# First normalisation of a two-layer hybrid trunk step, transposed before it is modulated

## The chip, the cores and the metric

One core of a Trainium2 chip runs the whole program. The metric is device time in microseconds. Engines are called PE (TensorE; PEld is its weight load), DVE (VectorE), ACT (ScalarE), POOL (GpSimd) and SP (SyncE); a name with a q behind it (SPq, ACTq) is that engine's sequencer, which issues DMAs.

## What is computed

Two trunk layers over 640 tokens (128 context tokens, 512 latent tokens) of width 1024. Each sub-layer begins with a normalisation and a modulation by learned columns, and its result goes through a projection. Only the first one matters here:

```python
def ada_params(cvec, w_mod, b_mod):
    m = jax.nn.silu(cvec) @ w_mod + b_mod
    return jnp.split(m[:, None, :], N_MOD, axis=-1)
...
hp = modulate(rmsnorm(xp, norm_mix_pre[layer]), mod_p[0], mod_p[1])   # x * (1 + scale) + shift
hs = modulate(rmsnorm(xs, norm_mix_pre[layer]), mod_s[0], mod_s[1])
u, v, gate, xr = jnp.split(h @ w_in, [D_A, 2 * D_A, 2 * D_A + D_RG], axis=-1)
```

The modulation vectors are `silu(c) @ w_mod`: a 1024 x 6144 weight per layer, of which shift and scale of the first sub-layer are 2 x 1024 columns, 8 MB. Context tokens and latent tokens have vectors of their own.

## The kernel before

`schedule()` writes out by hand one list of steps (`STEPS`) and one list of weight loads of 1 MB (`LOADS`). Each engine's block walks the whole list of steps in order and does its own part of each; semaphores join them. So the order of the list is the order of work on PE, DVE, ACT and POOL alike. SP walks the list of loads in order: a load that waits for its buffer holds all behind it.

**Products.** Large products are made in three passes (`split3`, L1146): an f32 operand is cut into a high part (fp32r) and a remainder, and high x high, high x remainder and remainder x high are accumulated. Weights are cut by `split`: ACT copies a block of 128 x 1024 to `WH` (L630), POOL subtracts it and writes `WL` (L854). `RING` holds 6 such blocks. A step's `split` list names the blocks cut behind it. Activations are cut alike into `HH` and `HL`, features on the partitions, 8 feature tiles by 640 tokens.

**Loads.** `RAW` has two buffers (`RAWN`). A load into a used one waits on SP until its old content is read: for a first half of modulation weights until PE has multiplied it (`mod_read`, L582), for a weight pair until POOL has cut it (`w_lo`, L586). Six loads behind the first two (`EARLY`, L397) go to memory that is free at the start and wait for nothing. The input tokens `X` are loaded from ACT's queue (L614, L615).

**Modulation.** A step `mod` (L1177) multiplies two loads (16 matmuls of 128 x 512 with 32 columns of weights), DVE copies the bank to `PART` (L932), and the step `modfin` transposes it on PE (L1210) and lets DVE sum it into `MODC` and add bias and gain (L948 to L957). Four such pairs, `mod(0, 0, 0)`, `mod(0, 0, 1)`, `mod(0, 1, 0)` and `mod(0, 1, 1)`, give shift (c = 0) and scale (c = 1) of the first sub-layer, in halves of 512 features.

**Normalisation.** `pre` (L674, L969) squares and sums a tile of 128 tokens on ACT (L681), takes the root (L682), and DVE scales the tile into `ACC` (L973). `T` (L974, L1212) transposes its 8 feature tiles on PE in two banks; DVE modulates the lower four out of PSUM into `HF` (L982), ACT the upper four (L695). `cut` (L684) casts them into `HH` on ACT (L700, L702); DVE and POOL write the remainders to `HL` (L988, L849). `HF` is one buffer, so tile t + 1 is modulated only when tile t is cut.

**The first pair.** `apair("xr", 0, ...)` multiplies two blocks of 128 columns of `w_in` with all tokens, in two ranges, 0:256 and 256:640, each over the whole K of 8 feature tiles: the first range when two token tiles are cut, placed between tiles 3 and 4; the second when all are. `apair("xr", 2, ...)` and `apair("gate", 0, ...)` follow.

In order, the list before begins:

```python
mod(0, 0, 0)
step("sheet", uses_m=1)
mod(0, 0, 1)
P_(0, 0)
mod(0, 1, 0)
P_(0, 1)
...
```

The steps that the prediction speaks of by line: L681, L682, L972, L973 (`pre`), L1221 (transposes of `T`), L1189 (`mod`), L1210 and L948 to L957 (`modfin`), L630 and L854 (weights cut), L988 and L849 (remainders), L1149 to L1151 (`split3`), L576 and L589 (SP's loads).

Of the kernel before, what the change touches and what calls it, by code (L numbers as in the profile page):

```python
# [28 lines left out]
RAWN = 2  # L29
RING = 6  # L30
# [6 lines left out]
def schedule():  # L37
# [32 lines left out]
    def mod(layer, c, half):  # L70
        flush()
        ld = load("mod", layer=layer, c=c, half=half, kh=0, n=cb[0])
        load("mod", layer=layer, c=c, half=half, kh=1, n=cb[0])
        step("mod", uses_m=1, layer=layer, c=c, half=half, ld=ld, n=cb[0])
        pend.append((layer, c, half, cb[0]))
        cb[0] += 1

    def apair(what, tile, src, col, part=None, ld=None, norm=0):

        if ld is None:  # L80
            ld = load("acols", src=src, col=col)
        j = loads[ld]["first"]
        if part == 0:
            return step("A", uses_a=0, what=what, tile=tile, j=j, parts=(0,), fin=False, norm=norm), ld
        return step("A", uses_a=2, frees=2, what=what, tile=tile, j=j, parts=(1,) if part == 1 else (0, 1), fin=True, norm=norm), ld

# [72 lines left out]


    mod(0, 0, 0)
    step("sheet", uses_m=1)
    mod(0, 0, 1)
    P_(0, 0)
    mod(0, 1, 0)
    P_(0, 1)
    P_(0, 2)
    mod(0, 1, 1)
    P_(0, 3)
    P_(0, 4)  # L170
    flush()
    steps[-1]["split"] = [0, 1]
    for t in range(TT):
        T_(0, t)
        if t == 4:
            steps[-1]["split"] = [2, 3, 4, 5]
        if t == 3:
            ld = apair("xr", 0, ("w_in",), 1536, 0)[1]
    step("lambda")
    apair("xr", 0, ("w_in",), 1536, 1, ld)  # L180
    apair("xr", 2, ("w_in",), 1536 + 256)
# [123 lines left out]
def hybrid_step(nc, A):  # L305
# [5 lines left out]
    with ctx:  # L311
# [11 lines left out]
        X = sb("X", [P, TT, D])  # L323
        EARLY_H = alias("EARLY_H", [P, 4, 2048])
        HH = sb("HH", [P, KD, TOK], f32r)
# [60 lines left out]
        PT_LOAD = next(i for i, ld in enumerate(LOADS) if ld.get("src") == ("w_out_odd",)) + 1  # L386
        PT = [RAW[:, PT_LOAD % RAWN, 512 * i:512 * i + 512] for i in range(4)]

# [5 lines left out]
        def k_tok(t):  # L394
            return KTOK[:, {0: 0, TT: 1}.get(t, 2 + t % 2), :]

        EARLY = {i: EARLY_H[:, i - RAWN, :] if i < RAWN + 4 else MX[:, 2048 * (i % 2):2048 * (i % 2) + 2048]  # L397
                 for i in range(RAWN, RAWN + 6)}


        early_in = [sem(f"early_in{i}") for i in range(6)]
        raw_in = [sem(f"raw_in{i}") for i in range(RAWN)]
        const_in = [sem(f"const_in{i}") for i in range(14)]
        w_hi, w_lo, mod_read = sem("w_hi"), sem("w_lo"), sem("mod_read")
# [120 lines left out]
        def raw_arrived(eng, ld):  # L525
            if ld in EARLY:
                eng.wait_ge(early_in[ld - RAWN], 16)
            else:
                eng.wait_ge(raw_in[ld % RAWN], 16 * ((ld - (len(EARLY) if ld >= RAWN else 0)) // RAWN + 1))

# [19 lines left out]
        def raw(i):  # L550

            return EARLY[i] if i in EARLY else RAW[:, i % RAWN, :]

# [18 lines left out]
        @block.sync  # L572
        def _(sp):
            for i, ld in enumerate(LOADS):
                if i in EARLY:
                    sp.dma_start(raw_dst(i, ld), dram_view(ld)).then_inc(early_in[i - RAWN], 16)  # L576
                    continue
                if i >= RAWN:

                    old = LOADS[i - RAWN - (len(EARLY) if i < 2 * RAWN + len(EARLY) else 0)]  # L580
                    if old["kind"] == "mod" and old["kh"] == 0:
                        sp.wait_ge(mod_read, old["n"] + 1)  # L582
                    elif old["kind"] == "mod":
                        upto(sp, m_ready, old["m"])
                    else:
                        sp.wait_ge(w_lo, old["first"] + 2)  # L586
                    if i == PT_LOAD + RAWN:
                        upto(sp, m_ready, PV_M[-1])
                sp.dma_start(raw_dst(i, ld), dram_view(ld)).then_inc(raw_in[i % RAWN], 16)  # L589

            for t in range(TT):
                sp.wait_ge(x_new, 3 * TT + t + 1)
                dst = A["y_prompt"][0] if t == 0 else A["y_sample"][0, (t - 1) * P:t * P, :]
                sp.dma_start(dst, X[:, t, :]).then_inc(stored, 16)
            sp.wait_ge(stored, 16 * (2 + TT))
            sp.wait_ge(k_out, 16)
# [3 lines left out]
        def _(act):  # L600
# [6 lines left out]

            xs = A["x_sample"][0].rearrange("(t p) n -> p t n", p=P)
            act.dma_start(CC[:, 0, :], A["c_ctx"].rearrange("(p k) -> p k", k=KD)).then_inc(const_in[3], 16)
# [3 lines left out]
            act.dma_start(IDN[:, :], A["ident"]).then_inc(const_in[5], 16)  # L613
            act.dma_start(X[:, 0, :], A["x_prompt"][0]).then_inc(const_in[0], 16)  # L614
            act.dma_start(X[:, 1:TT, :], xs).then_inc(const_in[1], 16)  # L615

# [16 lines left out]
            for s in STEPS:  # L633
# [40 lines left out]
                elif k == "pre":  # L674
                    ph, t = s["ph"], s["t"]
                    if ph:
                        act.wait_ge(x_new, (ph - 1) * TT + t + 1)
                    else:
                        act.wait_ge(const_in[0] if t == 0 else const_in[1], 16)
                        act.wait_ge(consts_made, 3)  # L680
                    link(nc.scalar.activation(JUNK, X[:, t, :], ACT.Square, accum_out=STAT[:, t, 3:4]))  # L681
                    nc.scalar.activation(STAT[:, t, 4:5], STAT[:, t, 3:4], ACT.Sqrt, scale=1.0 / D, bias=EPSC[:, :])\  # L682
                        .then_inc(xsum, 1)
                elif k == "cut":  # L684

# [17 lines left out]
                elif k == "A" and s["fin"]:  # L703
                    if s["what"] == "xr" and s["tile"] == 2:

                        input_ready(act, TT)
                        act.dma_start(WSR, A["gmlp_ws"][0].rearrange("h p q -> p h q")).then_inc(wst_in, 16)
# [84 lines left out]
                elif k == "Q":  # L792
                    u, i = s["m"], s["n"]
                    act.wait_ge(m_ready[u % 2], u // 2 + 1)
                    if i == 0:
                        input_ready(act, 3 * TT)
                    if i > 1:
# [61 lines left out]
        def _(dve):  # L859
# [40 lines left out]
            for s in STEPS:  # L900
# [241 lines left out]
        def _(pe):  # L1142
# [21 lines left out]

            RANGE = ((0, 256), (256, TOK))
            ntiles = ngate = 0
            for s in STEPS:
# [31 lines left out]
                elif k == "modfin":  # L1199
                    upto(pe, m_free, MOD_M[s["n"]])  # L1200
                    if s["c"] in (2, 5):
                        for v in (0, 1):
                            u = s["m"] + v
                            m_acquire(u)
                            MM(m_bank(u), SEL[:, v, :], PART[:, :], start=True, stop=True).then_inc(m_ready[u % 2], 1)
                    else:
                        u = s["m"]
                        m_acquire(u)
                        for i in range(4):
                            ins = TR(m_bank(u)[:, P * i:P * i + P], PART[:, P * i:P * i + P], IDN[:, :])  # L1210
                        ins.then_inc(m_ready[u % 2], 1)
                elif k == "T":  # L1212
                    ntiles += 1
                    t = s["t"]
                    pe.wait_ge(xn_ready, s["n"] + 1)
                    for q in (0, 1):
# [6 lines left out]
                elif k == "A":  # L1223

                    for part in s["parts"]:
                        if len(s["parts"]) == 1:
                            input_ready(pe, ntiles if part else TT * s["norm"] + 2)
                    if len(s["parts"]) == 2:
                        input_ready(pe, ntiles)
# [25 lines left out]
                elif k == "B":  # L1255
                    b, t, nb, what = s["b"], s["t"], s["nb"], s["what"]
                    b_acquire(b)
                    if what == "wout":
                        if s["ph"] == 1 and nb == 0:
                            pe.wait_ge(mix_lo, 4)  # L1260
                            upto(pe, m_free, YA_M[t])
                        if s["ph"] == 3:
                            upto(pe, m_free, PV_M[-2])
                            upto(pe, m_free, PV_M[-1])
                    elif what == "qkv":
                        input_ready(pe, 2 * TT + (t + 1 if nb == 2 else TT))
                    for kt in range(KD):
# [177 lines left out]
```

## Time and profile before

| | us |
|---|---|
| median of 3 runs (1629.41 to 1630.31) | 1629.56 |
| the profiled execution, its own time | 1628.96 |
| its span | 1627.2 |
| PE busy | 1506.1 (93%) |
| DVE / ACT / POOL busy | 656.2 / 554.5 / 518.1 |
| DMA moved | 153.87 MB, mean 95 GB/s |
| mean granted clock of PE | 0.968 |

The span runs from the first to the last instruction; the profiled execution's own time is 1.76 us more. In rows of the trace each line has its start and its busy time in us, the engine, the line of the kernel, the operation, the tiles it writes and reads (`out<-in`), how many instructions are merged in it (x4), and in brackets how long the engine was idle before it and what ended that. Granted clock 1.00 is 2.4 GHz, 0.50 is 1.2 GHz.

### The profile page before, as it was taken

What the parts mean: (1) busy time and instruction counts of PE and PEld (TensorE: products, weight loads), DVE (VectorE), ACT (ScalarE), POOL (GpSimd) and SP (SyncE); (2) the same over time, 40 slices, a digit from 0 to 9 for tenths busy, and PEclk for the clock granted to TensorE, in tenths of its full rate; (3) what the DMA queues carried; (4) which work ended last, traced back from release to release, by engine and by line L of the source; (5) the groups of instructions that cost most, each with busy time, mean ns of one, the idle gap of its engine ahead of it and who ended that gap; (6) DMA issues with size and microseconds to landing.
All of it is one profiled execution on the core that took longest, in us unless ns stands there. A gap on an engine that the chain in (4) does not pass through costs nothing.

```text
span 1627.2 us, 20069 instructions
## 1 busy us (share of the span) xinstructions
PE 1506.1 (93%) x8338; PEld 1242.4 (76%) x8338; DVE 656.2 (40%) x1124; ACT 554.5 (34%) x927; POOL 518.1 (32%) x224
## 2 busy tenths in 40 slices
PE   4799869899999999999889789989899999999997
PEld 1786646697898898998677656657689899989985
DVE  3665662733322322222644466623542232223225
ACT  3456732631221221232531266614532223222211
POOL 0521233141242243243234134413324234323330
PEclk9899979999999999999999899999899999999999
DMA  9322425144344342222022000033242122213201
GB/s 336 98 78 104 145 70 174 37 158 143 130 141 144 130 152 93 92 78 78 27 83 78 27 1 2 1 104 130 82 145 84 59 97 79 78 52 104 78 26 65
DMA packets 90498, 153.87 MB, mean 95 GB/s; under 512 B 6356, under 2 KB 44704, under 8 KB 90408
## 3 DMA queue, kind: packets, MB, share of 16 engines
q1 hardware_dynamic: 81712, 143.14, 26.7%
q10 hardware_dynamic: 8696, 9.45, 2.1%
q8 instruction: 66, 1.08, 0.3%
q14 instruction: 24, 0.20, 0.0%
HBM read 149.69 MB, written 2.89 MB: 94 GB/s over the span
## 4 chain that ended last, share of the span: by engine, by line
PE 71%; DVE 8%; ACT 5%; issue 2%; DMA 1%; POOL 1%; ACTq 0%; DVEq 0%; SPq 0%
PE PS L1149 20%; PE PS L1150 20%; PE PS L1151 20%; PE PS L1189 3%; PE PS L1387 2%; PE PS L1379 1%; DVE X L968 1%; DVE ACC L967 1%; PE PS L1357 1%; PE PS L1340 1%; PE PS L1358 1%; POOL WL L854 1%; ACT XCB L671 1%; DVE HL L988 1%; DVE HF L982 1%
## 5 line engine op out<-in xcount | busy, mean ns | idle before, releaser
L854 POOL TENSOR_TENSOR WL<-RAW,WH 128x1024 fp32r<-128x1024 f32 x172 | 422.0, 2484 | 769.2 <-ACT WH L630 769.2
L1149 PE MATMUL PS<-HH,WH 128*128 128x384 f32 (+1 forms) x1152 | 359.6, 312 | 10.4 <-DVE HL L988 5.3
L1151 PE MATMUL PS<-HH,WL 128*128 128x384 f32 (+1 forms) x1152 | 358.2, 311 | 0.0
L1150 PE MATMUL PS<-HL,WH 128*128 128x384 f32 (+1 forms) x1152 | 358.2, 311 | 0.0
L630 ACT CAST WH<-RAW 128x1024 fp32r<-128x1024 f32 x172 | 170.3, 1047 | 500.5 <-PE PS L1151 294.4
L1149 PE MATMUL PS<-WH,AH 128*128 128x512 f32 x640 | 253.3, 396 | 11.8 <-DVE AL L1003 6.5
L1150 PE MATMUL PS<-WL,AH 128*128 128x512 f32 x640 | 251.3, 393 | 0.0
L1151 PE MATMUL PS<-WH,AL 128*128 128x512 f32 x640 | 251.1, 392 | 0.0
L1149 PEld LDWEIGHTS PS<-HH,WH 128*128 128x128 f32 x1152 | 221.3, 192 | 16.1 <-issue 9.8
L1150 PEld LDWEIGHTS PS<-HL,WH 128*128 128x128 f32 x1152 | 221.5, 192 | 0.5
L1151 PEld LDWEIGHTS PS<-HH,WL 128*128 128x128 f32 x1152 | 220.9, 192 | 0.0
L1070 DVE TENSOR_TENSOR ACC<-ACC,PS 128x512 f32<-128x512 f32 x140 | 95.6, 687 | 233.3 <-PE PS L1151 233.3
L1001 DVE TENSOR_TENSOR XCB<-XCB 128x640 f32<-128x640 f32 x64 | 65.7, 1027 | 288.7 <-ACT XCB L718 288.5
L1149 PEld LDWEIGHTS PS<-WH,AH 128*128 128x128 f32 x640 | 121.1, 189 | 47.2 <-issue 8.6
L1149 PE MATMUL PS<-WH,HH 128*128 128x512 f32 x360 | 147.7, 410 | 8.7 <-POOL WL L854 5.4
L1150 PE MATMUL PS<-WL,HH 128*128 128x512 f32 x360 | 142.7, 396 | 0.0
L1151 PE MATMUL PS<-WH,HL 128*128 128x512 f32 x360 | 142.6, 396 | 0.0
L1151 PEld LDWEIGHTS PS<-WH,AL 128*128 128x128 f32 x640 | 121.3, 189 | 25.8
L1150 PEld LDWEIGHTS PS<-WL,AH 128*128 128x128 f32 x640 | 121.2, 189 | 24.7 <-issue 0.2
L718 ACT ACTIVATE XCB<-PS 128x640 f32<-128x640 f32 x64 | 45.1, 705 | 199.7 <-PE PS L1151 199.7
L1003 DVE TENSOR_TENSOR AL<-XCB,AH 128x640 fp32r<-128x640 f32 x64 | 76.7, 1198 | 50.7 <-ACT AH L724 50.7
L1149 PEld LDWEIGHTS PS<-WH,HH 128*128 128x128 f32 x360 | 69.1, 192 | 35.4 <-issue 10.9
(160 smaller groups left out, 1552.3 us busy)
## 6 DMA issues: line engine op xcount, KB each, us to landing
RAW<-in_w_mod SPq DMA_DIRECT2D x42, 1024.0 KB, 5.1
RAW<-in_w_ffn_in SPq DMA_DIRECT2D x32, 1024.0 KB, 5.7
RAW<-in_w_ffn_out SPq DMA_DIRECT2D x32, 1024.0 KB, 4.9
RAW<-in_w_in_even SPq DMA_DIRECT2D x8, 1024.0 KB, 6.8
RAW<-in_w_qkv SPq DMA_DIRECT2D x6, 1024.0 KB, 5.4
EARLY_H<-in_w_mod SPq DMA_DIRECT2D x4, 1024.0 KB, 21.2
RAW<-in_w_out_even SPq DMA_DIRECT2D x4, 1024.0 KB, 5.5
RAW<-in_w_out_odd SPq DMA_DIRECT2D x4, 1024.0 KB, 5.2
```

Of the source, the lines that this page charges most:

```text
L630: nc.scalar.copy(ring_view(WH, ld, j), w_view(ld, b)).then_inc(w_hi, 1)
L671: link(nc.scalar.activation(JUNK, ACC[:, t, :], ACT.Square, accum_out=STAT[:, t, 0:1]))
L718: nc.scalar.activation(XC[0], a_bank(a), ACT.Relu).then_inc(a_free[a % 2], 1)
L854: nc.gpsimd.tensor_tensor(ring_view(WL, ld, j), w_view(ld, b), ring_view(WH, ld, j).bitcast(f32), ALU.subtract).then_inc(w_lo, 1)
L1001: V_.tensor_tensor(XC[1], XC[0], XC[0], ALU.mult).then_inc(sq_ready, 1)
L1003: V_.tensor_tensor(AL[:, slot, :], XC[1], AH[:, slot, :].bitcast(f32), ALU.subtract).then_inc(a_lo, 1)
L1070: V_.tensor_tensor(acc, acc, bank, ALU.add).then_inc(b_free[b % 2], 1)
L1149: MM(out, wh, xh, start=first, stop=False)
L1150: MM(out, wh, xl, start=False, stop=False)
L1151: return MM(out, wl, xh, start=False, stop=last)
L1189: ins = MM(PS[32 * kt:32 * kt + 32, 6 + u % 2, :], CL[:, 4 * kh + kt, :], rv[:, kt, :], start=(kh == 0), stop=(kh == 1 and not gate))
L1387: ins = MM(PS[64 * par:64 * par + 64, 6 + u % 2, 0:256], vv(keys[kt])[:, HD * g:HD * g + HD], pt[:, par, :, :], start=(kt == 0), stop=(kt ...
```

## The change

The input tokens are loaded first, from SP's queue, tile by tile. Each tile is normalised as before and then transposed unmodulated: `xt` transposes its 8 feature tiles into two banks, DVE copies the lower four and ACT the upper four back to `ACC`. All five tiles come ahead of the modulation. Then the modulation pairs run in another order: first the lower half of the features (shift, scale), then the upper half. A new step `h0` per feature tile modulates all 640 tokens on DVE (two instructions, context and latent), casts on ACT and writes the remainder on DVE, in place of POOL and DVE by token tile. The first pair of products is made in two halves of K: `A0` over feature tiles 0 to 3 of block 0 ahead of the upper modulation pairs and of block 1 behind them, then tiles 4 to 7 of both (`kh=1`).

The list of loads becomes: 0, 1 (shift, lower), 2, 3 (scale, lower), 4 (the first `w_in` pair), 5, 6 (shift, upper), 7, 8 (scale, upper), 9 (next `w_in` pair), and so on. 2, 3, 5, 6, 7 and 8 are the ones with memory of their own; 0 and 1 take the two RAW buffers, 4 takes the buffer of 0, 9 that of 1.

```diff
+    for t in range(TT):
+        P_(0, t)
+        step("xt", t=t)
+    step("sheet", uses_m=1)
     mod(0, 0, 0)
-    step("sheet", uses_m=1)
+    mod(0, 1, 0)
+    flush()
+    ld = load("acols", src=("w_in",), col=1536)
+    steps[-1]["split"] = [0]
+    for f in range(4):
+        step("h0", f=f)
+    steps[-1]["split"] = [1]
+    step("A0", i=0, j=0)
     mod(0, 0, 1)
-    P_(0, 0)
-    mod(0, 1, 0)
-    P_(0, 1)
-    P_(0, 2)
     mod(0, 1, 1)
-    P_(0, 3)
-    P_(0, 4)
     flush()
-    steps[-1]["split"] = [0, 1]
-    for t in range(TT):
-        T_(0, t)
-        if t == 4:
-            steps[-1]["split"] = [2, 3, 4, 5]
-        if t == 3:
-            ld = apair("xr", 0, ("w_in",), 1536, 0)[1]
+    step("A0", i=1, j=0)
+    for f in range(4, KD):
+        step("h0", f=f)
+        steps[-1]["split"] = {5: [2], 6: [3], 7: [4, 5]}.get(f, [])
+    apair("xr", 0, ("w_in",), 1536, None, ld, kh=1)
     step("lambda")
-    apair("xr", 0, ("w_in",), 1536, 1, ld)
     apair("xr", 2, ("w_in",), 1536 + 256)
...
+        EARLY = {2: MX[:, 0:2048], 3: MX[:, 2048:4096],
+                 5: EARLY_H[:, HALF_H:HALF_H + 2048], 6: EARLY_H[:, 3 * HALF_H:3 * HALF_H + 2048],
+                 7: GGF[:, 0:2048], 8: GGF[:, 2048:4096]}
+        RAW_NO = {ld: r for r, ld in enumerate(i for i in range(len(LOADS)) if i not in EARLY)}
+        RAW_LD = sorted(RAW_NO)
...
+            for t in range(TT):
+                rows = A["x_prompt"][0] if t == 0 else A["x_sample"][0, (t - 1) * P:t * P, :]
+                sp.dma_start(X[:, t, :], rows).then_inc(x_in[t], 16)
             for i, ld in enumerate(LOADS):
                 if i in EARLY:
...
-                if i >= RAWN:
-
-                    old = LOADS[i - RAWN - (len(EARLY) if i < 2 * RAWN + len(EARLY) else 0)]
+                if RAW_NO[i] >= RAWN:
+
+                    old = LOADS[RAW_LD[RAW_NO[i] - RAWN]]
                     if old["kind"] == "mod" and old["kh"] == 0:
                         sp.wait_ge(mod_read, old["n"] + 1)
...
+                elif k == "xt":
+                    act.wait_ge(xt_mm, s["t"] + 1)
+                    nc.scalar.copy(ACC[:, s["t"], 512:1024], xt_banks(s["t"])[1]).then_inc(xt_hi, 1)
+                elif k == "h0":
+                    f = s["f"]
+                    act.wait_ge(h0_mod, f + 1)
+                    nc.scalar.copy(HH[:, f, :].rearrange("p (t n) -> p t n", t=TT), first_h(f)).then_inc(h0_hi, 1)
...
+                elif k == "xt":
+                    dve.wait_ge(xt_mm, s["t"] + 1)
+                    V_.tensor_copy(ACC[:, s["t"], 0:512], xt_banks(s["t"])[0]).then_inc(xt_lo, 1)
+                elif k == "h0":
+
+                    f = s["f"]
+                    dve.wait_ge(xt_lo if f < 4 else xt_hi, TT)
+                    for v, (t0, t1) in enumerate(((0, 1), (1, TT))):
+                        x = ACC[:, t0:t1, P * f:P * f + P]
+                        ins = V_.tensor_scalar(x, x, MODC[:, 0, 1, f, v:v + 1], MODC[:, 0, 0, f, v:v + 1], ALU.mult, ALU.add)
+                    ins.then_inc(h0_mod, 1)
+                    for g in ([f - 1] if f % 4 else []) + ([f] if f % 4 == 3 else []):
+                        dve.wait_ge(h0_hi, g + 1)
+                        V_.tensor_tensor(HL[:, g, :].rearrange("p (t n) -> p t n", t=TT), first_h(g),
+                                         HH[:, g, :].rearrange("p (t n) -> p t n", t=TT).bitcast(f32), ALU.subtract).then_inc(h0_lo, 1)
...
+            def first_rows(i, j, kts):
...
+                for kt in kts:
+                    pe.wait_ge(h0_lo, kt + 1)
+                    for c0, c1 in RANGE:
+                        ins = split3(a_bank(i)[:, c0:c1], (wh[:, kt, :], wl[:, kt, :]), (HH[:, kt, c0:c1], HL[:, kt, c0:c1]),
+                                     kt == 0, kt == KD - 1)
+                return ins
...
+                elif k == "xt":
+                    t = s["t"]
...
+                    pe.wait_ge(xn_ready, t + 1)
...
+                    for q in (0, 1):
+                        for i in range(4):
+                            f = 4 * q + i
+                            ins = TR(xt_banks(t)[q][:, P * i:P * i + P], ACC[:, t, P * f:P * f + P], IDN[:, :])
+                    ins.then_inc(xt_mm, 1)
+                elif k == "A0":
+
+                    i, j = s["i"], s["j"] + s["i"]
+                    pe.wait_ge(xt_lo, TT)
+                    pe.wait_ge(xt_hi, TT)
+                    pe.wait_ge(w_lo, j + 1)
+                    first_rows(i, j, range(0, 4))
...
+                    if s["kh"]:
+                        for i in (0, 1):
+                            first_rows(i, s["j"] + i, range(4, KD)).then_inc(a_ready[(s["a"] + i) % 2], 1)
+                        continue
```

## Rows read from the trace of the kernel before

**Rows 1.** Page, part 4: the chain that ended last, by engine

```profile
PE 71%; DVE 8%; ACT 5%; issue 2%; DMA 1%; POOL 1%; ACTq 0%; DVEq 0%; SPq 0%
```

**Rows 2.** Windows: length, busy us of each engine, then granted clock, DMA share, GB/s

```profile
20.00:30.00 10.00, 5.92 (x28) 1.44 (x28) 2.26 (x6) 5.14 (x12) 0.00 (x0) 1.00 1.06 384
...
60.00:70.00 10.00, 7.71 (x35) 7.74 (x36) 7.93 (x7) 6.09 (x9) 9.12 (x5) 0.83 0.26 62
```

**Rows 3.** Timeline of the first 34 us, all engines

```profile
8.69 0.22 ACT L619 ACTIVATE CSG<-CC 128x16 f32<-128x16 f32 x1
...
11.86 1.06 ACT L681 ACTIVATE XCB<-X 128x1024 f32<-128x1024 f32 x1 [2.95 <-DMA X<-in_x_prompt]
...
14.32 0.29 ACT L682 ACTIVATE STAT<-STAT,EPSC 128x1 f32<-128x1 f32 x1
...
19.70 1.06 ACT L681 ACTIVATE XCB<-X 128x1024 f32<-128x1024 f32 x1 [5.09 <-DMA X<-in_x_sample]
...
20.88 0.29 ACT L682 ACTIVATE STAT<-STAT,EPSC 128x1 f32<-128x1 f32 x1
...
33.57 1.07 PE L1189 MATMUL PS<-MX,CL 128*32 128x512 f32 x8 [1.55 <-DMA MX<-in_w_mod]
```

**Rows 4.** Timeline: second range of the first pair, start of the second pair

```profile
62.29 0.41 PE L1149 MATMUL PS<-HH,WH 128*128 128x384 f32 x1 [4.13 <-POOL HL L849]
...
72.28 0.28 PE L1149 MATMUL PS<-HH,WH 128*128 128x256 f32 x1
```

**Rows 5.** Timeline around 289 us: root, copy out of PSUM and scaling of a tile

```profile
288.71 0.30 ACT L682 ACTIVATE STAT<-STAT,EPSC 128x1 f32<-128x1 f32 x1
288.91 0.57 ACT L759 COPY ACC<-PS 128x512 f32<-128x512 f32 x1
...
289.23 0.76 DVE L973 TENSOR_SCALAR ACC<-X,STAT 128x1024 f32<-128x1024 f32 x1
```

**Rows 6.** Timeline of the first 36 us: modulation matmuls, PART, transposes, first sum

```profile
9.18 3.64 PE L1189 MATMUL PS<-RAW,CL 128*32 128x512 f32 x16 [9.18 <-DVE CL L873]
...
29.62 0.69 DVE L932 COPY PART<-PS 128x512 f32<-128x512 f32 x1 [2.57 <-PE PS L1189]
...
30.36 0.66 PE L1210 MATMUL PS<-IDN,PART 128*128 128x128 f32 x4 [0.88 <-DVE PART L932]
...
31.94 0.18 DVE L948 TENSOR_REDUCE MODC<-PS 128x8 f32<-128x32 f32 x1
...
35.51 1.11 PE L1210 MATMUL PS<-IDN,PART 128*128 128x128 f32 x4 [0.87 <-DVE PART L932]
```

**Rows 7.** Windows of PE alone: busy, granted clock, DMA share, GB/s

```profile
35.73:38.88 3.15, 2.71 (x12) 0.50 0.94 296
```

**Rows 8.** DMA issues of the first 120 us: size, median us from issue to landing

```profile
RAW<-in_w_mod SPq DMA_DIRECT2D x4, 1024.0 KB, 5.3
```

**Rows 9.** Groups by line and shape: busy us, mean ns of one, idle before, releaser

```profile
L854 POOL TENSOR_TENSOR WL<-RAW,WH 128x1024 fp32r<-128x1024 f32 x172 | 422.0, 2484 | 769.2 <-ACT WH L630 769.2
...
L630 ACT CAST WH<-RAW 128x1024 fp32r<-128x1024 f32 x172 | 170.3, 1047 | 500.5 <-PE PS L1151 294.4 <-DMA RAW<-in_w_ffn_in 143.4 <-DMA RAW<-in_w_out_odd 29.8
...
L1018 DVE TENSOR_TENSOR GG<-GG 128x640 f32<-128x640 f32 x8 | 6.6, 825 | 0.3
...
L485 DVE TENSOR_SCALAR XCB<-MX,PC 128x640 f32<-128x640 f32 x8 | 4.9, 610 | 9.5 <-ACT MX L712 9.4
...
L783 ACT CAST HH<-MX 128x640 fp32r<-128x640 f32 x4 | 2.6, 724 | 4.2 <-POOL MX L837 4.2
```

**Rows 10.** Timeline from 62 us on: POOL cuts four blocks, DVE's small operations beside it

```profile
62.11 9.42 POOL L854 TENSOR_TENSOR WL<-RAW,WH 128x1024 fp32r<-128x1024 f32 x4
...
62.21 2.31 DVE L912 TENSOR_TENSOR LG<-PC,LG 128x8 f32<-128x8 f32 x1
...
67.12 2.07 DVE L917 TENSOR_TENSOR LG<-LG 128x8 f32<-128x8 f32 x1
...
75.59 2.41 DVE L926 TENSOR_SCALAR NCL<-LG 128x8 f32<-128x8 f32 x1
```

More of the change, by code:

```diff
@@ L76, in mod, with apair @@
         cb[0] += 1
-    def apair(what, tile, src, col, part=None, ld=None, norm=0):
+    def apair(what, tile, src, col, part=None, ld=None, norm=0, kh=0):
         if ld is None:
@@ L83, in apair @@
         if part == 0:
-            return step("A", uses_a=0, what=what, tile=tile, j=j, parts=(0,), fin=False, norm=norm), ld
-        return step("A", uses_a=2, frees=2, what=what, tile=tile, j=j, parts=(1,) if part == 1 else (0, 1), fin=True, norm=norm), ld
+            return step("A", uses_a=0, what=what, tile=tile, j=j, parts=(0,), fin=False, norm=norm, kh=kh), ld
+        return step("A", uses_a=2, frees=2, what=what, tile=tile, j=j, parts=(1,) if part == 1 else (0, 1), fin=True, norm=norm, kh=kh), ld
     def bgroup(what, nb, t, j, ph=None):
@@ L323, in hybrid_step @@
         X = sb("X", [P, TT, D])
-        EARLY_H = alias("EARLY_H", [P, 4, 2048])
+        EARLY_H = alias("EARLY_H", [P, 2 * KD * TOK])
         HH = sb("HH", [P, KD, TOK], f32r)
@@ L386, in hybrid_step @@
         PT_LOAD = next(i for i, ld in enumerate(LOADS) if ld.get("src") == ("w_out_odd",)) + 1
-        PT = [RAW[:, PT_LOAD % RAWN, 512 * i:512 * i + 512] for i in range(4)]
+        PT = [RAW[:, (PT_LOAD - 6) % RAWN, 512 * i:512 * i + 512] for i in range(4)]
         def vv(t):
@@ L395, in k_tok @@
             return KTOK[:, {0: 0, TT: 1}.get(t, 2 + t % 2), :]
-        EARLY = {i: EARLY_H[:, i - RAWN, :] if i < RAWN + 4 else MX[:, 2048 * (i % 2):2048 * (i % 2) + 2048]
-                 for i in range(RAWN, RAWN + 6)}
-        early_in = [sem(f"early_in{i}") for i in range(6)]
+        HALF_H = KD * TOK // 2
+        EARLY = {2: MX[:, 0:2048], 3: MX[:, 2048:4096],
[3 more added lines that the diff above has]
+        RAW_LD = sorted(RAW_NO)
+        early_in = {i: sem(f"early_in{i}") for i in EARLY}
         raw_in = [sem(f"raw_in{i}") for i in range(RAWN)]
-        const_in = [sem(f"const_in{i}") for i in range(14)]
+        const_in = [sem(f"const_in{i}") for i in range(11)]
+        x_in = [sem(f"x_in{t}") for t in range(TT)]
+        xt_mm, xt_lo, xt_hi = sem("xt_mm"), sem("xt_lo"), sem("xt_hi")
+        h0_mod, h0_hi, h0_lo = sem("h0_mod"), sem("h0_hi"), sem("h0_lo")
         w_hi, w_lo, mod_read = sem("w_hi"), sem("w_lo"), sem("mod_read")
@@ L467, in hybrid_step, with xt_banks, first_h @@
         QKV_B = [s["b"] for s in STEPS if s["kind"] == "B" and s["what"] == "qkv"][-1]
+        def xt_banks(t):
+            return [PS[:, 2 * (t % 3) + q, :] for q in (0, 1)]
+        def first_h(f):
+            return ACC[:, :, P * f:P * f + P]
         def step_done(eng, s):
@@ L526, in raw_arrived @@
             if ld in EARLY:
-                eng.wait_ge(early_in[ld - RAWN], 16)
+                eng.wait_ge(early_in[ld], 16)
             else:
-                eng.wait_ge(raw_in[ld % RAWN], 16 * ((ld - (len(EARLY) if ld >= RAWN else 0)) // RAWN + 1))
+                eng.wait_ge(raw_in[RAW_NO[ld] % RAWN], 16 * (RAW_NO[ld] // RAWN + 1))
         def dram_view(ld):
@@ L550, in raw @@
         def raw(i):
-            return EARLY[i] if i in EARLY else RAW[:, i % RAWN, :]
+            return EARLY[i] if i in EARLY else RAW[:, RAW_NO[i] % RAWN, :]
         def raw_dst(i, ld):
@@ L573, in _ @@
         def _(sp):
+            for t in range(TT):
+                rows = A["x_prompt"][0] if t == 0 else A["x_sample"][0, (t - 1) * P:t * P, :]
+                sp.dma_start(X[:, t, :], rows).then_inc(x_in[t], 16)
             for i, ld in enumerate(LOADS):
                 if i in EARLY:
-                    sp.dma_start(raw_dst(i, ld), dram_view(ld)).then_inc(early_in[i - RAWN], 16)
+                    sp.dma_start(raw_dst(i, ld), dram_view(ld)).then_inc(early_in[i], 16)
                     continue
-                if i >= RAWN:
-                    old = LOADS[i - RAWN - (len(EARLY) if i < 2 * RAWN + len(EARLY) else 0)]
+                if RAW_NO[i] >= RAWN:
+                    old = LOADS[RAW_LD[RAW_NO[i] - RAWN]]
                     if old["kind"] == "mod" and old["kh"] == 0:
@@ L588, in _ @@
                         upto(sp, m_ready, PV_M[-1])
-                sp.dma_start(raw_dst(i, ld), dram_view(ld)).then_inc(raw_in[i % RAWN], 16)
+                sp.dma_start(raw_dst(i, ld), dram_view(ld)).then_inc(raw_in[RAW_NO[i] % RAWN], 16)
             for t in range(TT):
@@ L606, in link @@
                 act.wait_ge(act_done, own[0])
-            xs = A["x_sample"][0].rearrange("(t p) n -> p t n", p=P)
             act.dma_start(CC[:, 0, :], A["c_ctx"].rearrange("(p k) -> p k", k=KD)).then_inc(const_in[3], 16)
@@ L613, in _ @@
             act.dma_start(IDN[:, :], A["ident"]).then_inc(const_in[5], 16)
-            act.dma_start(X[:, 0, :], A["x_prompt"][0]).then_inc(const_in[0], 16)
-            act.dma_start(X[:, 1:TT, :], xs).then_inc(const_in[1], 16)
             act.wait_ge(const_in[3], 16)
@@ L678, in _ @@
                     else:
-                        act.wait_ge(const_in[0] if t == 0 else const_in[1], 16)
+                        act.wait_ge(x_in[t], 16)
                         act.wait_ge(consts_made, 3)
@@ L704, in _ @@
                     if s["what"] == "xr" and s["tile"] == 2:
-                        input_ready(act, TT)
+                        upto(act, m_ready, SHEET_M)
                         act.dma_start(WSR, A["gmlp_ws"][0].rearrange("h p q -> p h q")).then_inc(wst_in, 16)
@@ L795, in _ @@
                     if i == 0:
-                        input_ready(act, 3 * TT)
+                        input_ready(act, 2 * TT)
                     if i > 1:
@@ L1165, in _ @@
             RANGE = ((0, 256), (256, TOK))
+            def first_rows(i, j, kts):
+                wh = WH[:, j % RING, :].rearrange("p (k n) -> p k n", k=KD)
+                wl = WL[:, j % RING, :].rearrange("p (k n) -> p k n", k=KD)
+                for kt in kts:
[4 more added lines that the diff above has]
+                return ins
             ntiles = ngate = 0
@@ L1211, in _ @@
                         ins.then_inc(m_ready[u % 2], 1)
+                elif k == "xt":
+                    t = s["t"]
+                    if t == 0:
+                        pe.wait_ge(const_in[5], 16)
+                    pe.wait_ge(xn_ready, t + 1)
+                    if t > 2:
+                        pe.wait_ge(xt_lo, t - 2)
+                        pe.wait_ge(xt_hi, t - 2)
+                    for q in (0, 1):
[9 more added lines that the diff above has]
+                    first_rows(i, j, range(0, 4))
                 elif k == "T":
@@ L1214, in _ @@
                     t = s["t"]
-                    pe.wait_ge(xn_ready, s["n"] + 1)
+                    pe.wait_ge(xn_ready, TT + s["n"] + 1)
                     for q in (0, 1):
@@ L1226, in _ @@
                         if len(s["parts"]) == 1:
-                            input_ready(pe, ntiles if part else TT * s["norm"] + 2)
-                    if len(s["parts"]) == 2:
+                            input_ready(pe, ntiles if part else TT * (s["norm"] - 1) + 2)
+                    if s["kh"]:
+                        for i in (0, 1):
+                            first_rows(i, s["j"] + i, range(4, KD)).then_inc(a_ready[(s["a"] + i) % 2], 1)
+                        continue
+                    if len(s["parts"]) == 2 and s["norm"]:
                         input_ready(pe, ntiles)
@@ L1265, in _ @@
                     elif what == "qkv":
-                        input_ready(pe, 2 * TT + (t + 1 if nb == 2 else TT))
+                        input_ready(pe, TT + (t + 1 if nb == 2 else TT))
                     for kt in range(KD):
```

## The prediction

> **What bounds the kernel now.** I read the chain of waits first: PE holds 71% of it, and the rest lies at the seams between stages [rows 1]. The change touches only the first seam, so its gain or loss is the shift of one moment: when PE starts the second pair of products. From there every step, load and wait is the same in both kernels and hangs on its predecessor. Before, the second pair starts at 72.28 [rows 4].
>
> Then I read the windows and the timeline up to that moment. Until about 35 us the transfers bound: 384 GB/s with a DMA share of 1.06 [rows 2]; the last modulation matmuls wait for their load and start at 33.57 [rows 3]. After them the tiles go through a chain (transpose, modulate, cast, remainder); the second range waits 4.13 us for POOL's last remainder and starts at 62.29 [rows 4]. From 60 to 70 us PE is busy for 7.71 of 10 us, with transfers at 62 GB/s [rows 2]. So 33.57 to 72.28, 38.7 us, hold some 14 us of products at the fast clock and for the rest this chain. The change wants to move the transposes under the 35 us of transfers. The question is what that order makes the transfers and modulation wait for.
>
> **Part 1: the five tiles, now ahead of everything.** In the list, `pre(t)` and `xt(t)` alternate, and ACT does both. So ACT can't square tile t + 1 before it has copied tile t out of PSUM, which waits for PE, which waits for DVE's scaling, which waits for ACT's root. One tile after the other:
> - square to root: 19.70 to 20.88, 1.18 us [rows 3];
> - root to end of DVE's scaling: 288.71 to 289.23 + 0.76, 1.28 [rows 5];
> - 8 transposes: twice four. Four take 0.66 or 1.11 [rows 6]. I take 1.11, so 2.2: the slow one goes with a granted clock of 0.50 (1.2 GHz) in the stretch behind it [rows 7], and PE is idle for 3 of 5 us here. Before the clock's first change the rows show 1.00, yet the first 16 modulation matmuls take 3.64, where 8 later ones take 1.07 [rows 3, 6]: I read the start as slow too;
> - ACT's copy, 0.57 [rows 5].
> With some 0.1 of semaphores that is 5.3 us a tile. ACT starts at 8.69 + 0.22 = 8.9, when it has made the sigmoid; the first X tile, now first on SP, has landed by then (before it came at 11.86, behind weights). The first tile has a table load more: square to root 14.32 - 11.86 = 2.46 [rows 3], so 6.6. The last transposes end at 8.9 + 6.6 + 3 x 5.3 + 4.7 = 36.1.
>
> **Part 2: what is queued behind it.** PE's first modulation matmul stands behind all five tiles. SP needs its first half for load 4 (the first `w_in` pair takes the buffer of load 0 and waits for `mod_read`), and loads 5 to 9 are queued behind load 4. So the transfers do 2.6 MB of X and 4 MB of weights, idle from about 21 us (7.4 MB with the constants at 384 GB/s), and go on only when PE has multiplied load 0. That cover is spent.
> - `sheet`: 0.6. First modulation pair: 3.64 slow or 2.1 fast (2 x 1.07) [rows 3, 6]; PE has been busy since 34, so 3.0. DVE's `PART` 0.69, transposes 0.66 [rows 6].
> - Second pair 2.1, `PART` 0.69, transposes 0.66, then DVE's four small operations, 0.2 each like the first [rows 6]: 0.8. With semaphores, `h0` can start at 36.1 + 0.6 + 4.5 + 3.6 + 0.9 = 45.7.
> - Load 4 is issued at about 38.7 and lands 5.3 later [rows 8]: 44. Loads 5 to 9 follow 2.7 us apart (1.05 MB at 384 GB/s), the last at 57.5. Each is there before its use; I cost them at nothing, and with a landing 3 us later still nothing.
>
> **Part 3: `h0`, lower half.** Per feature tile DVE modulates 640 tokens: one instruction of that width takes 0.61, two about 0.75 (below by 0.61; above by 1.5, twice the 0.76 of [rows 5]). The remainder takes 0.82, ACT's cast 0.72 [rows 5, 9]. So DVE bounds, 1.57 a tile, and four take 6.4 with the last cast exposed in part. POOL cuts weight block 0 just then (load at 44, cast 1.05, POOL 2.48 [rows 9]). While POOL cut four blocks from 62.11 on, a DVE operation on 8 columns took 2.31 and another 2.07; at 75.59 one took 2.41 [rows 10]: such operations wait for POOL's to end. The price of block 0 is between 0 and 2.5; I take 1.5, as DVE mostly is not at its start. Lower half ready: 45.7 + 6.4 + 1.5 = 53.6. `A0` of block 0 runs along and ends 1.2 later (24 matmuls, 6 per feature tile, 0.9 fast, 1.6 slow): 54.8.
>
> **Part 4: upper modulation.** Twice 2.1 + 0.69 + 0.66 with semaphores 7.0, then 0.8: `h0` goes on at 62.6. Here the transfers hide nothing, as before these matmuls ran as their loads came. `A0` of block 1 (3.6) lies under `h0`.
>
> **Part 5: `h0`, upper half.** 6.4 again. Now POOL cuts blocks 2 and 3 in the middle (their casts are placed behind tiles 5 and 6): 0 to 5.0, and I take 3.2. Ready at 72.2. Then tile 7 of block 0, 0.9, and tiles 4 to 7 of block 1, 3.55: second pair at 76.6.
>
> **Removed:** the chain by token tile and the split by range, all inside the stretch to 72.28. **Behind:** `lambda` moves behind the pair; its DVE work and ACT's eight DMA issues lie under the second pair's 14 us, as its results are used only after the third; nothing, at most 1 us if the copy of the second pair waited for ACT. WSR, buffers and parities of later loads stay.
>
> **Sum:** 76.6 - 72.3 = +4.3 on 1628.96, that is 1633.2 for the profiled execution; the median of the runs is 0.6 higher, so 1633.8.
>
> **The page of the skill that bears on it.** POOL held DVE up in [rows 10]. The Trainium skill, "SBUF — State Buffer", has the reason in its rule on the port pair that DVE and GpSimd share: an exclusive lock, held for the whole instruction, the other fully blocked. By that rule none of `h0`'s operations gets through beside a cut, and it is the first rival below. Also, "TensorE: Matmul & The Clock Gate" says that the default state is throttled, and activity releases it; that speaks for the slow transposes of part 1, and no run here shows yet what these bursts do.
>
> **Rivals.**
> 1. **POOL and DVE take turns.** If POOL's next cut gets in after every single DVE operation, as in [rows 10], the two parts of tile 7's modulation are separated by a whole cut, and both halves pay in full: 2.5 and 5.0 in place of 1.5 and 3.2, 79.4: +7.1, 1636.7 (1636.1 if one DVE operation slips by). For it: the rows. Against it: POOL must have a block ready each time, and ACT's casts lie between `h0`'s own.
> 2. **The clock is fast under the transposes (not slower).** Its place is part 1: 8 transposes in 1.3, 0.9 less for each of five tiles, and the first modulation pair 0.9 less: 71.2, -1.1 and 1628.5. It decides at 0.86 a tile, where +4.3 is gone. For it: four transposes at 0.66 between two modulation pairs [rows 6]. Against: those came after a long busy stretch.
> 3. **No collision with POOL.** Loads or casts fall elsewhere: -4.7, 71.9, 1629.1, no difference.
> 4. **Both 2 and 3:** 66.5, -5.8, 1623.8: the change does what it is called, faster.
> 5. **A load is late after all** (part 2's estimate off by over 3 us at load 8): +3 on the forecast.
>
> **Numbers.** The forecast within 2 us has 0.45, rival 1 0.17, rival 2 0.12, rival 3 0.13, rival 4 0.08, rival 5 0.05. 0.2% is 3.3 us, about what a measurement of this kernel can tell from none: slower begins at 1632.8. Three quarters of the forecast (0.34), rivals 1 and 5 are slower: 0.55; the rest of the forecast and rivals 2 and 3: 0.36; faster 0.09. The range takes in rivals 1 to 3 with the error of their sums, 1627 to 1637. Cases of no difference lie close below, so beside it the forecast's own: 1631.8 to 1635.8.
>
> **What the changed profile would show.** ACT's squares (L681's) 5.3 us apart from 8.9 on, each behind a copy; no transfers from about 21 to 39 us; load 4 issued just when the first 8 modulation matmuls end; `h0` first at about 46, second half at 62 to 63; DVE operations of over 2 us beside POOL's cuts; second pair at 76.6. Squares 4.4 us apart would make the forecast wrong by rival 2; a second pair that waits for a load or a cut by rival 5; a shift of the second pair that the end doesn't show would break the reading that all behind it is the same.

## The result, and the profile after

| | before | changed |
|---|---|---|
| median of 11 runs, us | 1629.56 (1626.85 to 1631.75) | 1635.24 (1631.97 to 1636.29) |
| ratio to before | | 1.0030, 95% interval 1.0022 to 1.0037 |
| profiled execution: own time, span | 1628.96, 1627.2 | 1631.97, 1630.1 |
| second pair of products starts | 72.28 [rows 4] | 76.94 |

The change makes the kernel slower by 0.22 to 0.37%, 3.6 to 6.0 us. The profiled execution of the changed kernel is the fastest of its 11, so its span shows only part of it.

The first 77 us of the changed kernel, in windows (length; busy us of PE, PEld, DVE, ACT, POOL; granted clock; DMA share; GB/s): tiles and lower modulation, lower `h0` with `A0` of block 0, upper modulation, the rest of the pair.

```profile
0.00:41.50 41.50, 16.12 (x82) 10.11 (x82) 12.41 (x26) 12.76 (x24) 0.20 (x4) 1.00 0.61 214
41.50:53.20 11.70, 6.42 (x28) 6.20 (x30) 8.67 (x16) 4.65 (x6) 4.72 (x2) 0.56 1.06 382
53.20:60.60 7.40, 5.72 (x47) 2.54 (x47) 2.30 (x8) 0.00 (x0) 0.00 (x0) 1.00 0.58 188
60.60:77.10 16.50, 11.89 (x70) 11.25 (x69) 10.45 (x15) 7.33 (x9) 9.82 (x4) 0.90 0.22 67
...
22.00:36.00 14.00, 7.93 (x40) 5.19 (x39) 4.25 (x9) 4.44 (x9) 0.00 (x0) 1.00 0.02 7
```

No compute engine is busy throughout in any of them. The transfers are full from 41.50 to 53.20 (382 GB/s), but PE waits for no load there. In the 14 us of the last line, a part of the first window, the transfers stand still, where the kernel before moved 384 GB/s [rows 2]. Why is seen in its timeline (start, busy us, engine, line):

```profile
7.62 1.06 ACT L698 ACTIVATE XCB<-X 128x1024 f32<-128x1024 f32 x1
...
13.48 0.59 ACT L703 COPY ACC<-PS 128x512 f32<-128x512 f32 x1 [3.11 <-PE PS L1274]
...
13.96 1.06 ACT L698 ACTIVATE XCB<-X 128x1024 f32<-128x1024 f32 x1
...
18.97 1.06 ACT L698 ACTIVATE XCB<-X 128x1024 f32<-128x1024 f32 x1
...
31.48 1.97 PE L1274 MATMUL PS<-IDN,ACC 128*128 128x128 f32 x8 [3.03 <-DVE ACC L997]
...
33.72 2.87 PE L1240 MATMUL PS<-RAW,CL 128*32 128x512 f32 x16
...
35.71 0.37 SPq L609 DMA_DIRECT2D RAW<-in_w_in_even  x1
...
41.26 1.04 ACT L647 CAST WH<-RAW 128x1024 fp32r<-128x1024 f32 x1 [7.19 <-DMA RAW<-in_w_in_even]
...
42.19 3.54 DVE L1007 TENSOR_SCALAR ACC<-ACC,MODC 128x128 f32<-128x128 f32 x4
42.39 2.35 POOL L878 TENSOR_TENSOR WL<-RAW,WH 128x1024 fp32r<-128x1024 f32 x1 [41.95 <-ACT WH L647]
```

From the second on, ACT's squares (L698) come 5.01 us apart, each behind the copy (L703) of the tile before. PE multiplies the first modulation weights at 33.72, though the transfers had all but stopped at 22, and load 4 is issued only when their first half has been multiplied, at 35.71. When it lands, its cut on POOL falls on the first modulation of `h0`: four instructions take 3.54.

The other end of the stage, by engine (DVE, POOL, PE):

```profile
60.67 1.52 DVE L1007 TENSOR_SCALAR ACC<-ACC,MODC 128x128 f32<-128x128 f32 x4
...
63.02 0.80 DVE L1007 TENSOR_SCALAR ACC<-ACC,MODC 128x128 f32<-128x128 f32 x2
...
64.47 4.90 DVE L1007 TENSOR_SCALAR ACC<-ACC,MODC 128x128 f32<-128x128 f32 x2
69.29 1.69 DVE L1011 TENSOR_TENSOR HL<-ACC,HH 128x640 fp32r<-128x640 f32 x2
...
63.98 5.10 POOL L878 TENSOR_TENSOR WL<-RAW,WH 128x1024 fp32r<-128x1024 f32 x2 [11.03 <-ACT WH L647]
...
70.16 0.58 PE L1188 MATMUL PS<-HH,WH 128*128 128x256 f32 x1 [4.40 <-DVE HL L1011]
...
76.94 0.28 PE L1188 MATMUL PS<-HH,WH 128*128 128x256 f32 x1
```

The two modulation instructions of tile 6 take 0.80, the same two of tile 7 take 4.90. POOL's two cuts run from 63.98 to 69.08; in narrower windows the second cut is seen to start between 66.4 and 66.8, the second DVE instruction between 66.5 and 67.0. So the first instruction waited for the first cut and got in before the second, and the other waited for the second. PE waits 4.40 for the remainder behind them. The Trainium skill ("SBUF — State Buffer", "Who interferes with whom") calls the port pair that DVE and GpSimd share an exclusive lock, held for the whole instruction. The trace agrees: 4.90 beside two cuts, 0.80 without.

### The profile page after: what moved, and what is told of

Read it like the earlier page. It is cut to its first block, busy times and chain, and to the rows that moved or that the text cites. A ratio compares the mean times of both kernels' runs of the same rounds, so it can differ in the third digit from the quotient of the medians.

```text
span 1630.1 us, 20041 instructions
## 1 busy us (share of the span) xinstructions
PE 1503.5 (92%) x8338; PEld 1245.1 (76%) x8338; DVE 658.4 (40%) x1128; ACT 550.6 (34%) x910; POOL 512.0 (31%) x219
## 4 chain that ended last, share of the span: by engine, by line
PE 71%; DVE 8%; ACT 5%; issue 2%; POOL 1%; DMA 0%; ACTq 0%; DVEq 0%
PE PS L1188 21%; PE PS L1189 20%; PE PS L1190 20%; PE PS L1240 2%; PE PS L1462 2%; PE PS L1454 1%; DVE X L992 1%; DVE ACC L991 1%; PE PS L1432 1%; PE PS L1415 1%; PE PS L1433 1%; POOL WL L878 1%; ACT XCB L688 1%; DVE HL L1027 1%; DVE RAW L521 1%
```

## The experiments

The times are medians. The changed kernel ran beside the kernel before at 1629.56, the others in two later groups, beside it at 1630.16 in both. So a difference from the changed kernel that is taken between medians, as below, would be 0.6 us more if it were taken by the ratios. "Seam" is the start of the second pair in the profiled execution.

| kernel | seam | median | ratio to before, 95% interval |
|---|---|---|---|
| changed | 76.94 | 1635.24 | 1.0030 (1.0022 to 1.0037) |
| tiles' squares one ahead | 64.57 | 1622.53 | 0.9955 (0.9941 to 0.9969) |
| cuts of blocks 2, 3 later | 71.84 | 1628.58 | 0.9994 (0.9985 to 1.0003) |
| load 4 in its own memory | 76.43 | 1632.74 | 1.0014 (1.0005 to 1.0022) |
| all three | 58.45 | 1614.36 | 0.9901 (0.9888 to 0.9915) |
| pair in one go | 78.59 | 1634.87 | 1.0032 (1.0019 to 1.0044) |
| all three, modulation first | 56.73 | 1615.09 | 0.9908 (0.9895 to 0.9921) |
| the same, both cuts first | 56.53 | 1612.51 | 0.9895 (0.9881 to 0.9908) |

### Squares one tile ahead

```diff
     for t in range(TT):
         P_(0, t)
-        step("xt", t=t)
+        if t:
+            step("xt", t=t - 1)
+    step("xt", t=TT - 1)
```

> Edit: on every engine the squares and scaling of tile t + 1 come ahead of the transposes' copies of tile t; nothing else. Theory (ACT's order makes the tiles a chain of 5.0 us each, and PE's first modulation matmul waits behind it): the tiles come 2.5 us apart, the last transposes end at about 23.6 in place of 33.4, everything behind shifts with them, second pair at about 67 in place of 76.9; 9.8 less than the changed kernel, about 1625.5. Rival (the start is bound by transfers or by PE's slow transposes): at most 2 less, second pair at 75 or later.

The timeline: ACT's squares, PE's last transposes and its first modulation matmuls:

```profile
10.45 1.04 ACT L700 ACTIVATE XCB<-X 128x1024 f32<-128x1024 f32 x1
...
14.14 1.06 ACT L700 ACTIVATE XCB<-X 128x1024 f32<-128x1024 f32 x1
...
15.99 1.06 ACT L700 ACTIVATE XCB<-X 128x1024 f32<-128x1024 f32 x1
...
21.66 1.10 PE L1276 MATMUL PS<-IDN,ACC 128*128 128x128 f32 x8 [1.19 <-DVE ACC L999]
...
22.87 1.92 PE L1242 MATMUL PS<-RAW,CL 128*32 128x512 f32 x16
```

The squares come 1.9 to 3.7 apart, 2.8 in the mean, and the modulation starts at 22.87 in place of 33.72. The seam moves 12.4 us, and the time is 12.7 less than the changed kernel's. Of the 2.6 at the seam beyond the 9.8 expected, 0.9 is there when the last transposes end (22.76) and 1.1 more when `h0` starts (30.38): PE does the first 16 modulation matmuls in 1.92, not 2.87. In this execution the last 8 transposes take 1.10, not 1.97. The order of the list was the chain; the rival falls.

### Cuts of blocks 2 and 3 behind tile 7

```diff
-        steps[-1]["split"] = {5: [2], 6: [3], 7: [4, 5]}.get(f, [])
+        steps[-1]["split"] = {7: [2, 3, 4, 5]}.get(f, [])
```

> Edit: the cuts of weight blocks 2 and 3 come behind feature tile 7 of h0, not behind 5 and 6. Theory (POOL's two cuts hold up the second of tile 7's two modulation instructions, and PE's wait for it lets its clock fall): tile 7's modulation takes 0.8 in place of 4.9, PE doesn't wait 4.4 us, second pair at 71.5, 5.4 less than the changed kernel, about 1629.8. Rival (PE will then wait for the cuts of blocks 2 and 3, which come later): the second pair starts no sooner than before, under 2 less.

```profile
64.84 0.80 DVE L1007 TENSOR_SCALAR ACC<-ACC,MODC 128x128 f32<-128x128 f32 x2
...
67.42 9.47 POOL L878 TENSOR_TENSOR WL<-RAW,WH 128x1024 fp32r<-128x1024 f32 x4 [14.17 <-ACT WH L647]
...
71.84 0.28 PE L1188 MATMUL PS<-HH,WH 128*128 128x256 f32 x1
```

Tile 7's modulation takes 0.80 in place of 4.90, the seam moves 5.1 us (5.4 expected), and the time is 6.7 less. The second pair waits for no cut. This edit alone brings the change back to no difference from before.

### Load 4 in its own memory

```diff
+        EARLY_W = alias("EARLY_W", [P, RING * 1024])
         WH = sb("WH", [P, RING, 1024], f32r)
...
-        EARLY = {2: MX[:, 0:2048], 3: MX[:, 2048:4096],
+        EARLY = {2: MX[:, 0:2048], 3: MX[:, 2048:4096], 4: EARLY_W[:, 4096:6144],
...
                     step_done(act, freed_by)
+                    if j in (4, 5):
+                        act.wait_ge(w_lo, 2)
```

The new memory lies in ring blocks 4 and 5, so the casts into these blocks wait until load 4 has been cut (the last two lines). A buffer number further on moves by one, as one load fewer goes through `RAW`.

> Edit: load 4 (first w_in pair) gets memory of its own (ring blocks 4 and 5), so SP waits for nothing before load 9 and the transfers don't stop at 22 us. Theory (each load comes before its use anyway): only block 0's cut moves ahead and no longer holds up h0's first modulation (3.54 for four instructions becomes 1.5): 2.0 less, second pair at 75, about 1633.2. Rival (the 15 us without transfers are what costs): 8 or more less, about 1627.

```profile
35.12 2.35 POOL L881 TENSOR_TENSOR WL<-EARLY_W,WH 128x1024 fp32r<-128x1024 f32 x1 [34.68 <-ACT WH L650]
...
42.77 1.52 DVE L1010 TENSOR_SCALAR ACC<-ACC,MODC 128x128 f32<-128x128 f32 x4
...
68.33 0.58 PE L1191 MATMUL PS<-HH,WH 128*128 128x256 f32 x1 [4.39 <-DVE HL L1014]
...
76.43 0.28 PE L1191 MATMUL PS<-HH,WH 128*128 128x256 f32 x1
```

The cut of block 0 now comes at 35.12, the first modulation of `h0` takes 1.52, and PE's last wait ends at 68.33 in place of 70.16, 1.8 sooner. The seam shows 0.5 of it in this execution: the mean granted clock from 66 to 78 us is 0.72 here and 0.86 in the changed kernel. The time is 2.5 less; the intervals of the two ratios just touch, so this is the least certain of the three gains. But 8 or more less is excluded: the 14 us without transfers cost no more than this, and as the main cause they fall.

### All three

> The three edits together. Theory (three separate costs that add): 9.8 + 5.4 + 2.0 less, second pair at about 60, about 1618, 0.993 of the kernel before. Rival (one cause behind them, or the transfers as a floor once the tiles are quick): no more than e1 alone gives, about 1625.

```profile
20.73 1.97 PE L1279 MATMUL PS<-IDN,ACC 128*128 128x128 f32 x8 [0.31 <-DVE ACC L1002]
...
22.97 2.93 PE L1245 MATMUL PS<-RAW,CL 128*32 128x512 f32 x16
...
27.65 2.23 DVE L981 TENSOR_TENSOR MODC<-MODC,BC 128x8 f32<-128x8 f32 x1
...
58.45 0.28 PE L1193 MATMUL PS<-HH,WH 128*128 128x256 f32 x1
```

Seam 58.45, 18.5 less than the changed kernel; time 20.9 less (17.2 expected), 15.8 less than the kernel before beside it. The three single edits gave 12.7 + 6.7 + 2.5 = 21.9. They are three costs, nearly additive, and not one cause. Two details qualify this. The tiles stand in the same order as in the first experiment, yet here the last 8 transposes and the first 16 modulation matmuls run at the slow clock (1.97 and 2.93), and the transposes still end at 22.70. So the fast clock there is no fixed part of that experiment's gain. And block 0's cut, now at 27.49, falls on an addition on 8 columns (2.23), which delays the copy of the next modulation bank by some 0.6.

### The pair in one go

```diff
-    step("A0", i=0, j=0)
...
-    step("A0", i=1, j=0)
...
-                            first_rows(i, s["j"] + i, range(4, KD)).then_inc(a_ready[(s["a"] + i) % 2], 1)
+                            pe.wait_ge(w_lo, s["j"] + i + 1)
+                            first_rows(i, s["j"] + i, range(0, KD)).then_inc(a_ready[(s["a"] + i) % 2], 1)
```

> From the changed kernel: the steps A0 are gone and the first pair is multiplied over all of K at the end (the halves of K undone, all else kept). Theory (A0 of block 0 holds PE's upper modulation matmuls until h0's lower half is done, and what it saves at the end it costs there): upper h0 starts 3 to 4 sooner, at 56.5 to 58, but seven more groups of products lie behind the last feature tile; second pair between 75.5 and 78, within 1.5 of the changed kernel, about 1635. Rival (the halves of K are a gain by themselves): 5 or more slower, about 1641.

```profile
57.73 1.51 DVE L1005 TENSOR_SCALAR ACC<-ACC,MODC 128x128 f32<-128x128 f32 x4
...
78.59 0.28 PE L1186 MATMUL PS<-HH,WH 128*128 128x256 f32 x1
```

Upper `h0` starts 2.9 sooner (57.73 against 60.67), the seam comes 1.7 later, a little past the bounds I set, in a profiled execution that is the slowest of the kernel's six (1638.72). The median, 1634.87, is not told apart from the changed kernel's. The halves of K neither make the loss nor, within a measurement's error, win anything in this place.

### Upper modulation first, and both cuts first

From the kernel with all three edits:

```diff
-    for f in range(4):
-        step("h0", f=f)
-    steps[-1]["split"] = [1]
-    step("A0", i=0, j=0)
     mod(0, 0, 1)
+    for f in (0, 1):
+        step("h0", f=f)
     mod(0, 1, 1)
+    for f in (2, 3):
+        step("h0", f=f)
+    steps[-1]["split"] = [1]
     flush()
+    step("A0", i=0, j=0)
     step("A0", i=1, j=0)
```

> From the kernel with all three edits: the upper modulation pairs are put between h0's lower tiles (one ahead of tiles 0 and 1, one ahead of 2 and 3) and A0 of both blocks behind them. Theory (part 4 of the prediction: behind A0, the 7 us of upper modulation are bare, though their loads have landed by 36): h0 goes from tile 3 to tile 4 with only the modulation's tail between, second pair at 52 to 54 in place of 58.5, 5 less, about 1609.5. Rival (loads 5 to 8 land too late for it, or DVE's own work bounds both): under 1.5 less.

```profile
29.54 1.07 PE L1247 MATMUL PS<-EARLY_H,CL 128*32 128x512 f32 x8 [0.92 <-DMA EARLY_H<-in_w_mod]
...
37.59 1.06 PE L1247 MATMUL PS<-GG,CL 128*32 128x512 f32 x8 [1.56 <-DMA GG<-in_w_mod]
...
43.58 2.24 DVE L987 SCALAR_TENSOR_TENSOR MODC<-MODC,PC 128x4 f32<-128x4 f32 x1
...
45.93 1.51 DVE L1014 TENSOR_SCALAR ACC<-ACC,MODC 128x128 f32<-128x128 f32 x4
...
56.73 0.28 PE L1195 MATMUL PS<-HH,WH 128*128 128x256 f32 x1
```

A miss: the seam gained 1.7, not 5, and the time (1615.09) is no different. The rival was right, in both of its halves. PE now waits for each load, the last until 37.59: up to there the transfers are the floor. PE still ends the last modulation matmuls 6.7 sooner than with all three edits (38.65 against 45.39), but upper `h0` starts only 1.7 sooner (45.93 against 47.66). The other 5.0 go to DVE: it does `h0`'s tiles 2 and 3 ahead of the modulation's last sum, and then the cut of block 1 holds a step of that sum for 2.24. No run took these two apart.

The second edit puts blocks 0 and 1 into one `split` ahead of `h0`:

```diff
-    steps[-1]["split"] = [0]
+    steps[-1]["split"] = [0, 1]
...
-    steps[-1]["split"] = [1]
```

> The kernel with the modulation pairs moved, and block 1 of the weights cut together with block 0, ahead of h0, so that no cut lies beside h0. Theory (each cut beside h0 costs DVE up to one cut, 2.3): 1 to 2.3 less than that kernel, about 1608. Rival (with ACT's casts between, POOL's cut of block 1 falls where DVE waits for nothing of it): no difference, within 0.5.

```profile
28.67 4.67 POOL L884 TENSOR_TENSOR WL<-EARLY_W,WH 128x1024 fp32r<-128x1024 f32 x2 [28.23 <-ACT WH L653]
...
31.09 2.27 DVE L986 SCALAR_TENSOR_TENSOR MODC<-MODC,PC 128x4 f32<-128x4 f32 x1
...
56.53 0.28 PE L1194 MATMUL PS<-HH,WH 128*128 128x256 f32 x1
```

The collision only moved: now the lower modulation's step on 4 columns takes 2.27. The seam is 0.2 sooner; the median is 2.6 less, but the intervals overlap, and the seam doesn't explain it, so I count it as not told apart. The three kernels that hold all three edits are the fastest, 0.9 to 1.1% under the kernel before; their intervals overlap.

## Why the prediction was right

1633.8 was forecast, range 1627 to 1637, and 1635.24 measured; forecast +4.3 at the seam, measured +4.66. The range is wide enough to hold the cases of no difference too; slower, which came true, had 0.55. By its steps:

| step | forecast | measured |
|---|---|---|
| ACT starts | 8.9 | 7.62 |
| a tile | 5.3 | 5.01 |
| last transposes end | 36.1 | 33.45 |
| load 4 issued | 38.7 | 35.71 |
| `h0` starts | 45.7 | 42.19 |
| lower half ready | 53.6 | 50.42 |
| `A0` of block 0 ends | 54.8 | 53.2 |
| upper `h0` starts | 62.6 | 60.67 |
| upper half ready | 72.2 | 71.0 |
| second pair | 76.6 | 76.94 |

- **Part 1**, the tile chain, was right: transposes slow, each tile behind the last, worth 12.7 us by the run that broke it. ACT started 1.3 earlier than forecast: its wait for the load of `CC` ended at 6.08, in the kernel before at 7.40. That wasn't weighed, and no run shows why the load landed sooner.
- **Part 2** was right: the transfers stop and it costs nothing directly. What it cost came through block 0's cut, part 3: 2.0 of 3.54, where 1.5 was taken.
- **Part 3, `A0` of block 0, was mis-sized**: 1.2 was taken from the lower half's end to its own, and 2.8 measured. PE had waited 5.32 for the first remainder; then the 24 matmuls took 6.42 (46.78 to 53.20) at a mean granted clock of 0.53, so PE ran behind DVE by the end.
- **Part 5**: the wait beside POOL was rival 1's pattern for tile 7: 4.90 where 0.80 is free, 4.1, above the 3.2 taken and below the 5.0. Rival 1's mechanism is in this kernel, POOL's next cut behind a single DVE operation. Its price of 7.5 for both halves was too high, and the forecast's 4.7 as much too low: 6.1 measured (4.1 + 2.0).
- **The end was mis-sized**: 4.4 forecast from the upper half's end to the seam, 6.0 measured. Two things: at 70.16 six groups of products were left, not five, since tile 6's remainder stood on DVE behind tile 7's blocked modulation; and PE had waited 4.40, and the granted clock is 0.50 from 70.16 to 71.92. At `h0`'s start the kernel was 3.5 ahead of the forecast, by the sooner start, 0.3 a tile and a modulation 0.9 shorter. `A0` (1.6), the upper half (0.7), the end (1.6) and the lower half (0.3) gave it back, less 0.3 at the upper modulation. That these errors cancel to 0.3 at the seam is luck; the agreement is better than its terms. What held is the order of the waits.
- **"From there everything is the same"** holds for instructions, not for times. The same DVE instructions (the last state copy of the first recurrence tile, then the X of the first token tile in three later stages) stand in the two profiled executions at:

before

```profile
124.76 0.15 DVE L881 COPY NS<-GG 128x1 f32<-128x1 f32 x1
...
286.26 1.23 DVE L968 TENSOR_TENSOR X<-X,ACC 128x1024 f32<-128x1024 f32 x1
...
782.54 1.22 DVE L968 TENSOR_TENSOR X<-X,ACC 128x1024 f32<-128x1024 f32 x1
...
1125.01 1.23 DVE L968 TENSOR_TENSOR X<-X,ACC 128x1024 f32<-128x1024 f32 x1
```

changed

```profile
131.06 0.15 DVE L905 COPY NS<-GG 128x1 f32<-128x1 f32 x1
...
293.06 1.22 DVE L992 TENSOR_TENSOR X<-X,ACC 128x1024 f32<-128x1024 f32 x1
...
787.63 1.22 DVE L992 TENSOR_TENSOR X<-X,ACC 128x1024 f32<-128x1024 f32 x1
...
1128.34 1.23 DVE L992 TENSOR_TENSOR X<-X,ACC 128x1024 f32<-128x1024 f32 x1
```

The shift is 4.7 at the seam, then 6.3, 6.8, 5.1, 3.3. At the first step, windows of the same work (each starts where the shift is 4.7 and ends where it is 6; PE alone: busy, granted clock, DMA share, GB/s) show a slow stretch that only the changed kernel has:

changed

```profile
104.70:121.00 16.30, 13.58 (x68) 0.90 0.20 65
121.00:184.00 63.00, 57.32 (x278) 0.97 0.31 105
```

before

```profile
100.00:115.00 15.00, 12.28 (x69) 1.00 0.22 71
115.00:178.00 63.00, 55.92 (x281) 1.00 0.31 106
```

The same work takes 1.3 us more there, at 0.90 against 1.00. Each kernel's runs spread over some 4 to 5 us, and the mean granted clock of 21 runs of the kernel before goes from 0.961 to 0.971, so one span can't be read to 2 us. I read the later steps of the shift alike, by argument; no run took them apart.

## What to carry to other kernels

In a list of steps that every engine walks in order, moving work "under" a transfer is worth its own chain first: count what one tile costs when the engine at both ends of the tile (here ACT, square and copy) can't start the next, and let it run one step ahead. Look for the load whose buffer is freed by what now stands behind that chain. Put POOL's cuts where DVE works out of PSUM or not at all; two cuts in a row beside one DVE chain hold it for both. And expect a cut that is moved to meet other DVE work: in three of the kernels here it did.

## What was not expected of the hardware

- After a POOL cut one waiting DVE instruction got in before POOL's next one, every time it was seen: tile 7's two instructions, 0.8 us of work, took 4.90, 4.90, 4.89 and 4.89 in the four kernels that cut there. Instructions on 4 columns waited as long (2.24 and 2.27 in the last two kernels). The modulation's sum, whose input is in PSUM, wasn't held: in the last kernel it took 0.19 at 29.66, between the start and the end of POOL's cuts (28.67 to 33.34), as without a cut.
- The gap in the transfers, the largest change that the profile shows (7 GB/s for 14 us), was worth least: 2.5 us, and what the trace shows of that is a collision on another engine.
- The same order of transposes ran at either clock: with the tiles 2.8 apart, the last 8 took 1.10 in one kernel and 1.97 in another, and both ended at about 22.7. In the changed kernel, with the tiles 5.0 apart, each 8 took 1.94 to 1.97.
